# Thirty-four of 128 expert tiles multiplied in pairs by seven block products, in a kernel that splits float32 in two

## What is computed

```python
def peer_experts(xc, idx, gates, u, v):
    u_sel = jnp.take(u, idx, axis=0)
    act = jax.nn.gelu(jnp.einsum("chkd,cd->chk", u_sel, xc))
    v_sel = jnp.take(v, idx, axis=0)
    return jnp.einsum("chk,chkd->cd", act * gates, v_sel)
```

## Time and profile before

| what | value |
|---|---|
| median of 3 runs | 1355.82 us (1354.9 to 1355.88) |
| the profiled execution's own time | 1356.69 us |
| its span in the profile | 1354.8 us |
| mean granted clock of TensorE | 0.994 of 2.4 GHz |
| TensorE busy | 98% of the span |
| VectorE, ScalarE, GpSimd busy | 70%, 57%, 33% |
| V stage | from about 989 to 1348 us |
| DMA in the V stage | 0.56 of 16 engines, 187 GB/s |

### The profile page before, as it was taken

The page is one execution under the profiler, slowest core; times in us unless marked ns, Lnnn a source line. Parts: engine busy times, 40 slices in busy tenths (PEclk is TensorE's granted clock), DMA queues, the critical chain, the costliest instruction groups (busy, mean ns, idle before and its releaser), DMA issues.

```text
span 1354.8 us, 26681 instructions
## 1 busy us (share of the span) xinstructions
PE 1330.0 (98%) x9169; PEld 1209.8 (89%) x9169; DVE 950.2 (70%) x1751; ACT 768.5 (57%) x1379; POOL 442.6 (33%) x254
## 2 busy tenths in 40 slices
PE   7999999999998999999999999999999999999997
PEld 7998979988978988999999999999988888888886
DVE  4777667656676974899989888889545555555555
ACT  6545454444556355477767676676545555555554
POOL 1100424000025661079887666766720000000000
PEclk9989999999999999999999999999999999999999
DMA  8533035555553444555554444444455555555553
GB/s 303 165 109 110 32 125 194 188 190 192 188 173 127 155 141 140 164 166 184 187 185 157 156 144 155 155 151 147 165 190 188 186 186 186 187 187 187 190 188 130
DMA packets 62465, 225.29 MB, mean 166 GB/s; under 512 B 7200, under 2 KB 7712, under 8 KB 62000
## 3 DMA queue, kind: packets, MB, share of 16 engines
q1 hardware_dynamic: 60656, 218.36, 48.6%
q10 hardware_dynamic: 1728, 5.84, 1.2%
HBM read 223.12 MB, written 1.05 MB: 165 GB/s over the span
## 4 chain that ended last, share of the span: by engine, by line
PE 95%; DVE 2%; issue 1%; ACT 1%; DMA 0%; POOL 0%; SPq 0%; POOLq 0%; DVEq 0%; ACTq 0%
PE bank L533 83%; PE bank L1072 3%; PE bank L634 1%; PE bank L780 1%; PE bank L766 1%; PE bank L590 1%; PE bank L1027 1%; DVE arena L2083 0%; PE bank L935 0%; DMA cols<-in_cols 0%; PE bank L565 0%; PE bank L515 0%; PE bank L950 0%; PE bank L682 0%; PE bank L595 0%
## 5 line engine op out<-in xcount | busy, mean ns | idle before, releaser
L1165 ACT ACTIVATE w_hi<-ring 128x1024 fp32r<-128x1024 f32 x414 | 439.2, 1061 | 515.5 <-PE bank L533 327.4
L1717 DVE TENSOR_TENSOR w_lo<-ring,w_hi 128x1024 fp32r<-128x1024 f32 x259 | 317.4, 1226 | 274.3 <-ACT w_hi L1165 269.7
L533 PE MATMUL bank<-hT_hi,w_hi 128*128 128x256 f32 (+2 forms) x1696 | 420.6, 286 | 0.0
L533 PE MATMUL bank<-hT_lo,w_hi 128*128 128x256 f32 (+2 forms) x1696 | 412.9, 282 | 0.0
L1669 POOL TENSOR_TENSOR w_lo<-ring,w_hi 128x1024 fp32r<-128x1024 f32 x128 | 310.4, 2427 | 158.3 <-ACT w_hi L1165 158.1
L533 PEld LDWEIGHTS bank<-hT_lo,w_hi 128*128 128x128 f32 x1696 | 320.4, 189 | 0.4
L533 PEld LDWEIGHTS bank<-hT_hi,w_hi 128*128 128x128 f32 x1696 | 318.9, 188 | 0.4
L533 PE MATMUL bank<-hT_hi,w_lo 128*128 128x256 f32 (+2 forms) x1696 | 234.8, 280 | 0.0
L533 PEld LDWEIGHTS bank<-hT_hi,w_lo 128*128 128x128 f32 x1696 | 215.9, 189 | 0.0
L533 PE MATMUL bank<-w_hi,wgt_lo 128*128 128x512 f32 x504 | 199.6, 396 | 0.0
L533 PE MATMUL bank<-w_hi,wgt_hi 128*128 128x512 f32 x504 | 199.3, 395 | 0.0
(11 more groups left out here) (360 smaller groups left out, 1683.2 us busy)
## 6 DMA issues: line engine op xcount, KB each, us to landing
ring<-in_stream SPq DMA_DIRECT2D x414, 512.0 KB, 3.5
arena<-in_rows ACTq DMA_DIRECT2D x1, 1536.0 KB, 10.8
consts<-in_consts ACTq DMA_DIRECT2D x1, 1152.0 KB, 5.6
arena<-in_keys ACTq DMA_DIRECT2D x1, 1024.0 KB, 6.1
h<-in_x SPq DMA_DIRECT2D x2, 256.0 KB, 3.8
h<-in_x ACTq DMA_DIRECT2D x2, 256.0 KB, 4.3
arena<-in_rows ACTq DMA_DIRECT2D x1, 512.0 KB, 3.5
out_h<-arena SPq DMA_DIRECT2D x2, 256.0 KB, 2.1
```

The costliest lines, as they stand in the source:

```text
L533: mm = nc.tensor.matmul(o, a, b, start=first and not low_part and xp is x[0], stop=last and low_part)
L1165: nc.scalar.activation(w_hi[:, g % S, :], ring[:, g % R, :], ACT.Copy).then_inc(hi_done, 1)
L1717: nc.vector.tensor_tensor(w_lo[:, g % S, :], ring[:, g % R, :], w_hi[:, g % S, :].bitcast(F32), ALU.subtract).then_inc(lo_done, 1)
```

## The change

Tiles 24+6k and 25+6k, for k = 0 to 16, are taken as pairs. A pair is a 2 x 2 block product: token blocks x two tiles of experts times two tiles x two column halves. Instead of eight block products of three matmuls it does seven (a Winograd form of Strassen's scheme): a11·W11, S1·T1, X3·T3, a12·W21, X4·W22, X2·T2, a22·T4. S1, X2, X3 and X4 are sums of blocks of weighted activations (128 x 128), T1 to T4 sums of blocks of the tiles (128 x 512). Four of the seven gather in banks 4 to 7 over all pairs, three in banks 0 to 2; after the last pair (tiles 120 and 121) eight sums on DVE and one copy on ACT bring banks 4 to 7 into `h`. The other 94 tiles are plain, four between two pairs, and alone use the slots of `ring`, `w_hi` and `w_lo` and the count g. A pair's tiles are loaded apart (`pair_load`, two DMAs) into `pair_w` (W11, W21, W22, W12); all buffers of the pairs lie where older data are dead.

The sums for pair k+1 and their splits are made during pair k and the four plain tiles behind it. With n0 the first tile of pair k, each engine does, beside the plain work:

- ACT: after the high rows of n0+2 the high parts of T1 and T3, then of the blocks W; after those of n0+3 the high parts of T2 and T4, then of the S and X.
- DVE: behind step n0-1 the sums T1 and T3; n0: T2; n0+1: X3 and S1; n0+2: the low parts of T1, T3, the sum T4, X2 and X4; n0+3: the low parts of the W, then of T2, T4; n0+4: the low parts of the S and X. (Read with k+1's sums: `beside` gives the next pair's number.)
- SP: the two loads of pair k+2 before the ring's load of n0+10, once the low parts of the W of pair k+1 are made.

The raw sums T and S, X of pair 0 are spread over steps 15 to 23. On TensorE the zeros that open the sums go (the first matmul of a bank has the start flag), and from tile 12 on the order is written out on all engines instead of looped. The load of the last row of gains moves on ACT from a wait behind step 123 to behind the copy of bank 6. The diff, without the list of semaphores taken over from earlier stages:

```diff
+PLAIN_BETWEEN = 4
+FIRST_PAIR = 24
+PAIRS = list(range(FIRST_PAIR, N_KEYS - 7, 2 + PLAIN_BETWEEN))
+PAIR_OF = {n + j: k for k, n in enumerate(PAIRS) for j in range(2)}
+PLAIN = [n for n in range(N_KEYS) if n not in PAIR_OF]
+G_OF = {n: G_V + at for at, n in enumerate(PLAIN)}
+G_LAST = G_V + len(PLAIN)
+V_LOOPED = 3
+def pair_beside(n, step):
+    at = n - step + PLAIN_BETWEEN + 2
+    return PAIRS.index(at) if at in PAIRS[1:] else None
+def first_beside(n, step):
+    return 0 if n == FIRST_PAIR - PLAIN_BETWEEN - 2 + step else None
+def beside(n, step, first_step):
+    k = first_beside(n, first_step)
+    return pair_beside(n, step) if k is None else k
...
+        X3, S1, X2, X4 = range(4)
+        T1, T3, T2, T4 = range(4)
+        W11, W21, W22, W12 = range(4)
...
+            g_looped = (G_V + PAIRS[0] - PLAIN_BETWEEN - 2 * R) // R * R
+            with sp_eng.Fori(1, g_looped // R) as i:
                 for s in range(R):
                     sp_eng.wait_ge(lo_done, i * R + (s - R + 1))
                     sp_eng.dma_start(ring[:, s, :], stream_in[bass.ds(i * R + s, 1), :, :].rearrange("a p n -> p (a n)"))\
                           .then_inc(slot_full[s], 16)
-            for g in range(G_END // R * R, G_END):
+            def pair_load(k):
+                first, second = (stream_in[G_V + PAIRS[k] + j] for j in range(2))
+                sp_eng.dma_start(pair_w[:, W11:W12 + 1:W12 - W11, :], first.rearrange("p (c n) -> p c n", c=2))\
+                      .then_inc(pair_loaded, 16)
+                sp_eng.dma_start(pair_w[:, W21:W22 + 1, :], second.rearrange("p (c n) -> p c n", c=2))\
+                      .then_inc(pair_loaded, 16)
+            sp_eng.wait_ge(wgt_out, 8)
+            pair_load(0)
+            for n in PLAIN:
+                g = G_OF[n]
+                if g < g_looped:
+                    continue
+                k = beside(PLAIN[g - G_V - R], 4, 4)
+                if k is not None and k + 1 < len(PAIRS):
+                    sp_eng.wait_ge(pair_lo, pair_lo0 + 2 + 4 * k)
+                    pair_load(k + 1)
                 sp_eng.wait_ge(lo_done, g - R + 1)
-                sp_eng.dma_start(ring[:, g % R, :], stream_in[g]).then_inc(slot_full[g % R], 16)
+                sp_eng.dma_start(ring[:, g % R, :], stream_in[G_V + n]).then_inc(slot_full[g % R], 16)
...
-            open_sums()
-            with pe.Fori(0, N_KEYS // PEER_BODY - 1) as i:
+            def pair_products(k):
+                n0, first, last = PAIRS[k], k == 0, k == len(PAIRS) - 1
+                def high(b, x, w):
+                    nc.tensor.matmul(bank[b][:, :], x[0], w, start=first and b >= 4, stop=False)
+                    nc.tensor.matmul(bank[b][:, :], x[1], w, start=False, stop=False)
+                def low(b, x, w):
+                    return nc.tensor.matmul(bank[b][:, :], x[0], w, start=False, stop=last and b >= 4)
...
+                pe.wait_ge(wgt_out, n0 + 1)
+                pe.wait_ge(pair_lo, pair_lo0 + 2 + 4 * k)
+                high(4, a11, pair_w_hi[:, W11, :])
+                low(4, a11, pair_w_lo[:, W11, :]).then_inc(pair_used, 1)
+                pe.wait_ge(pair_lo, pair_lo0 + 4 + 4 * k)
+                high(5, s1, pair_t_hi[:, T1, :])
+                low(5, s1, pair_t_lo[:, T1, :])
+                high(7, x3, pair_t_hi[:, T3, :])
+                low(7, x3, pair_t_lo[:, T3, :]).then_inc(pair_used, 1)
+                pe.wait_ge(wgt_out, n0 + 2)
+                high(0, a12, pair_w_hi[:, W21, :])
+                low(0, a12, pair_w_lo[:, W21, :])
+                high(1, x4, pair_w_hi[:, W22, :])
+                low(1, x4, pair_w_lo[:, W22, :]).then_inc(pair_used, 1)
+                high(6, x2, pair_t_hi[:, T2, :])
+                low(6, x2, pair_t_lo[:, T2, :])
+                high(2, a22, pair_t_hi[:, T4, :])
+                low(2, a22, pair_t_lo[:, T4, :]).then_inc(pair_used, 1)
...
+            for n in range(V_LOOPED * PEER_BODY, N_KEYS - 2):
+                if n in PAIRS:
+                    pair_products(PAIR_OF[n])
+                elif n in G_OF:
+                    plain_tile(n)
+            closing_rows([(G_OF[n], [wgt_lhs(n, t) for t in range(NT)], (wgt_out, n + 1))
                           for n in (N_KEYS - 2, N_KEYS - 1)], 0, 3)
...
-            with act.Fori(0, N_KEYS // PEER_BODY - 1) as i:
+            def rows_free(n):
+                if n - 2 in G_OF:
+                    act.wait_ge(tiles_done, G_OF[n - 2] + 1)
+                else:
+                    k = PAIR_OF[n - 2]
+                    act.wait_ge(pair_used, pair_used0 + 4 * k + (1 if n - 2 in PAIRS else 4))
+            def rows_high(n):
+                rows_free(n)
+                wgt_high(n, n)
+            def pair_copy(o, src):
+                nc.scalar.activation(o, src, ACT.Copy).then_inc(pair_hi, 1)
+            def pair_free(k, part):
+                if k:
+                    act.wait_ge(pair_used, pair_used0 + 4 * (k - 1) + part)
+            def w_copy(k):
+                act.wait_ge(pair_loaded, pair_loaded0 + 32 * (k + 1))
+                pair_free(k, 3)
+                pair_copy(pair_w_hi[:, :, :], pair_w[:, W11:W22 + 1, :])
+            def t_copy(k, first, sums, part):
+                act.wait_ge(pair_sums, pair_sums0 + sums + 6 * k)
+                pair_free(k, part)
+                pair_copy(pair_t_hi[:, first:first + 2, :], pair_t[:, first:first + 2, :])
+            def x_copy(k):
+                act.wait_ge(pair_sums, pair_sums0 + 6 + 6 * k)
+                pair_free(k, 4)
+                pair_copy(pair_x_hi[:, :, :], pair_x[:, :, :])
+            with act.Fori(0, V_LOOPED) as i:
                 for j in range(PEER_BODY):
                     hi(G_V + j + S, i, PEER_BODY)
                     act.wait_ge(tiles_done, i * PEER_BODY + (G_V + j + 1))
                     nc.scalar.activation(wgt_hi[:, j % 2, :],
                                          act_all[:, bass.ds(i * PEER_BODY + (j + 2), 1), :].rearrange("p a t -> p (a t)"),
                                          ACT.Copy).then_inc(wgt_step, 1)
-            act.wait_ge(wgt_out, N_KEYS - PEER_BODY)
-            act.dma_start(rows[:, 0, :], rows_in[0:1, 3 * D:4 * D].rearrange("a n -> (a n)").partition_broadcast(P))\
-               .then_inc(final_in, 16)
-            for n in range(N_KEYS - PEER_BODY, N_KEYS - 2):
-                hi(G_V + n + S)
-                act.wait_ge(tiles_done, G_V + n + 1)
-                wgt_high(n, n + 2)
+            for n in range(V_LOOPED * PEER_BODY + 2, N_KEYS):
+                if n in G_OF and n - 2 not in PAIR_OF:
+                    hi(G_OF[n])
+                if n in PAIRS:
+                    hi(G_OF[n + 2])
+                rows_high(n)
+                if n - 1 in PAIRS:
+                    hi(G_OF[n + 2])
+                k = beside(n, 2, -2)
+                if k is not None:
+                    t_copy(k, T1, 1, 2)
+                k = beside(n, 2, -1)
+                if k is not None:
+                    if k == 0:
+                        act.wait_ge(wgt_out, 14)
+                    w_copy(k)
+                k = beside(n, 3, 0)
+                if k is not None:
+                    t_copy(k, T2, 4, 4)
+                k = beside(n, 3, 3)
+                if k is not None:
+                    if k == 0:
+                        act.wait_ge(wgt_out, 22)
+                    x_copy(k)
+                if n == PAIRS[-1] + 3:
+                    pair_copy(pair_t[:, T1, :], bank[6][:, :])
+                    act.dma_start(rows[:, 0, :], rows_in[0:1, 3 * D:4 * D].rearrange("a n -> (a n)").partition_broadcast(P))                       .then_inc(final_in, 16)
...
+            def pair_sum(o, a, b, op, k=0, needs=None):
+                if needs is not None:
+                    dve.wait_ge(pair_sums, pair_sums0 + needs + 6 * k)
+                nc.vector.tensor_tensor(o, a, b, op).then_inc(pair_sums, 1)
+            def pair_low(k, step, o, src, high):
+                dve.wait_ge(pair_hi, pair_hi0 + step + 4 * k)
+                nc.vector.tensor_tensor(o, src, high.bitcast(F32), ALU.subtract).then_inc(pair_lo, 1)
+            def t_low(k, step, first):
+                both = slice(first, first + 2)
+                pair_low(k, step, pair_t_lo[:, both, :], pair_t[:, both, :], pair_t_hi[:, both, :])
+            def first_sums(k):
+                dve.wait_ge(pair_loaded, pair_loaded0 + 32 * (k + 1))
+                pair_sum(pair_t[:, T1:T3 + 1, :], pair_w[:, W11:W22 + 1:2, :], over(pair_w[:, W12, :], 2), ALU.add)
...
+            def first_further(k):
+                pair_sum(pair_t[:, T2, :], pair_t[:, T1, :], pair_w[:, W22, :], ALU.add, k, 1)
+            def row_sums(k):
+                a11, a21, a12, a22 = rows_blocks(k)
+                if k:
+                    dve.wait_ge(pair_lo, pair_lo0 + 4 * k)
+                both = act_blocks[:, 2 * PAIRS[k]:2 * PAIRS[k] + 4:3, :]
```

(114 more changed lines are left out.)

13 lines of the change are left out of this document (7 added, 6 removed).

## The result

| | before | after |
|---|---|---|
| median | 1355.88 us (7 runs, 1353.86 to 1356.75) | 1347.44 us (7 runs, 1346.11 to 1351.69) |
| profiled execution, span | 1354.8 us | 1346.6 us |
| V stage, from its first matmul's start to its last one's | 989.09 to 1347.52: 358.4 us | 988.30 to 1339.03: 350.7 us |

The ratio is 0.9944, with an interval of 0.9931 to 0.9958: 5.7 to 9.4 us faster, 7.6 at the middle; the medians themselves differ by 8.4. The forecast was 1345.7, in a range of 1342.8 to 1351.5: the direction holds and the median lies in the range, 1.7 us above the forecast.

The account below looks back on a forecast made before the run. TensorE was taken as the bound, with 1.15 us of room a tile on DVE. The sum -11.9 - 0.9 + 2.1 + 0.6 = -10.1 us from 1355.8 gave 1345.7 us, range 1342.8 to 1351.5.

Parts of the forecast that it names:

- TensorE's saving: V stage: three matmuls fewer in each of 17 pairs, 11.9 us, and four opening matmuls on zeros gone, 0.9 us.
- the wait at the third plain tile: Each period: DVE's unbroken run makes TensorE wait 0.13 us before tile n0+4, 16 times, 2.1 us.
- The loads: Each pair's two-tile load lands in 4.9 us (bounds 3.4 and 6.1), in time for the next pair.
- a room of 0.45: Steady period: the pair's load, taken at 4.9 us, could land 0.45 us later without delaying the next pair.
- the 5.35: Landing time of a pair's load, in us, from which every period grows by the excess.
- The rival of the late load: Pair's load lands in 5.35 us or more, every period grows; 1349.5 us at 5.6, 1357.5 at 6.1; chance 0.14.
- First pair and end: Pair 0's sums delay steps 19 to 22 by 0.6 us once (0 to 1); the last eight sums are hidden.
- SP's wait for the W holds back no load that was due: SP's queue: waiting for the low parts of W before a pair's load delays no ring load; no cost.
- DVE never late: Rival: distances on DVE a shade shorter, so no wait at the third plain tile; 1343.3 us; chance 0.17.
- No overlap on DVE: Rival: DVE operations lose their 0.09 us overlap, the stall becomes 0.91 us a period; 1359.1 us; chance 0.06.

Follow-up runs that it names:

- experiment 7: Product a12*W21 left out of every pair, on the kernel of experiment 3: median 1345.51 us, period 16.22 us.
- 5: One more DVE subtraction of 256 elements ahead of the low parts of W, on the kernel of experiment 3: median 1350.84 us, period 16.556 us.
- experiment 4: Edits of experiment 2 and experiment 3 together on the changed kernel, pair 0's low parts of T2 and T4 at step 21: 1343.36 us, ratio 0.9919.
- experiment 2: DVE's low parts of T2 and T4 moved from step n0+3 to n0+4, against the changed kernel: 1348.16 us, ratio 0.9943.
- experiment 8: SP also waits for the low parts of T2 and T4 before loading the next pair, on the kernel of experiment 3: 1359.54 us, ratio 1.0028.
- experiment 3: SP issues pair 0's load two ring loads later and pair 1's one earlier, against the changed kernel: 1345.92 us, ratio 0.9933.

## Why the prediction was right, and what it missed

**TensorE's saving.** 11.9 + 0.9 us was forecast. From the last matmul of the U stage to the first of the V stage it is 0.12 us instead of 0.80. Before, that first matmul was a drawn-out one as well (0.59 us, the others 0.39; the next start 0.43 behind it), 0.2 more, so that the 0.9 is right. The products saved a little more than 11.9: a pair takes 1127.63 - 1122.77 = 4.86 us, not 4.90, which is 0.7 us over 17 pairs.

**The schedule, and the wait at the third plain tile.** Place, releaser and price were right: 0.13 us forecast, and the period came out at 16.23. The changed kernel's own profile names no releaser there; that of experiment 7 names DVE's low rows, and the times in 5 agree. Since the pairs are 0.04 us shorter the wait is 0.17 us against a period without it (16.05 in experiment 4), so the period agrees to 0.01 us partly because these two errors cancel. Experiments 2 and 4 take it away by DVE's order alone, 5 lengthens it one to one, 7 shows that TensorE's work is no longer what counts there.

**The loads.** The forecast had 4.9 us for two tiles in a row and a room of 0.45. In the steady stretch the first landed 3.9 to 4.2 us after its issue; the second was issued 0.6 us behind it and landed 4.6 to 4.9 us after that: 5.3 us for both in the mean, from 5.2 to 5.5. That is at the 5.35 from which the prediction's own sum has every period grow. Nothing grew because two other terms were too long: SP issues the load 0.03 us behind the low parts of W, not 0.15, and experiment 8 gives 2.75 us behind the start of the sum, not 2.95. The room that is left is 0.27 us by that experiment. That the load did not count in the steady period is thus in part luck. The rival of the late load was the right thing to fear, and it came true in another place.

**First pair and end: the step that failed.** "I count 0.2 + 0.4 = 0.6 us once (0 to 1)" held for tiles 21 and 22 (0.6 measured), but all waits before pair 0 come to 2.4 us. The sentence "SP's wait for the W holds back no load that was due" was reasoned for the steady period only, and the first two loads were given no price. Pair 0's load stands in SP's queue ahead of the ring load of tile 10 and waits until the rows of tile 7 are split; then its two DMAs are issued first. SP's queue at that point, in the changed kernel:

```profile
1007.12 0.65 SPq L526 DMA_DIRECT2D arena<-in_stream  x1
...
1007.82 0.58 SPq L528 DMA_DIRECT2D arena<-in_stream  x1
...
1008.45 9.87 SPq L542 DMA_DIRECT2D ring<-in_stream  x6
```

Tile 10 arrives too late, which costs 0.6 us. Pair 1's load stands behind the ring load of tile 27 and is issued at 1047.76; it lands at 1054.41, and DVE, which waits for it, gets to the rows of pair 0 too late, which costs 1.2 us. Moving both (experiment 3) brings 1.8 and 1.6 us by the V stage. With the measured terms the sum is -12.6 - 0.9 + 2.7 + 0.6 + 1.8 = -8.4 us, against 8.2 us by which the spans differ and the 10.1 that were forecast. Why single executions reach 1351 us is not shown: none of those was profiled.

**Rivals.** DVE never late: no, but experiment 4 makes it true. No overlap on DVE: out by the starts 1.14 us apart, in line with the rows of before and against the rule of the Trainium skill (VectorE: DVE Perf Modes, The DRAIN you can't avoid) that was weighed there. The same section adds that a next operation that is not held starts earlier, and the starts here agree with that. Late load: real, once, at pair 0.

## What to carry to other kernels

When work is moved under a bound engine, write out one period start by start from the profile's distances: here that gave eleven starts within 0.05 us and the one place where DVE's work is not hidden behind TensorE's. Then do the same for the first and the last round, queue by queue, since the DMA queue's order there is another one. And when the work is late by a tenth of a microsecond in each round, look first for work in that run that nobody needs yet: one operation moved behind the late one took away the whole wait of the steady period.

## What was not expected of the hardware

- A gap of 2.6 us on TensorE was followed by a stretch at the lower clock level, 1.2 GHz, which cost 1.6 us more (experiment 2, one execution). Gaps of 0.6 to 1.2 us in the changed kernel's profile left the clock at 1.00.
- SP's instruction for one tile took 0.33 us for the ring and 0.55 to 0.65 us for each of a pair's two loads, whose rows go to SBUF in two pieces of 2 KB; once it took 1.13 us (experiment 2).
- The 21 matmuls of a pair came 0.231 us apart (4.86 us a pair), those of plain tiles 0.233 us.
